# A two-block transformer forward pass: value weights applied to the latent keys ahead of the attention loop, and a new order of weight slots

## The reference, cut to what matters

```python
    c = rmsnorm(ckv, b_kv_norm[l])                      # (b, length, 256)
...
        p = jax.nn.softmax(s, axis=-1)
        o_lat = jnp.einsum('bhqk,bqkc->bqhc', p.astype(g.dtype), g)
        outs.append(jnp.einsum('bqhc,hcd->bqhd', o_lat, w_uv))
    ...
    h = h + jnp.concatenate([o_a, o_b], axis=-1) @ w_out[l]
```

## Time and profile before

| | |
|---|---|
| median of 3 runs | 1381.53 us (1381.42 to 1381.89) |
| the profiled execution: its own time | 1376.42 us |
| its span, first to last instruction | 1374.5 us |
| mean granted TensorE clock | 0.934 |
| PE busy | 1218.1 us (89% of the span) |
| DVE, ACT, POOL busy | 441.1, 391.6, 29.8 us |
| read from device memory | 320.09 MB, 235 GB/s over the span |
| attention loop of the first block with what stands around it | about 360 to 420 us |
| expert stages | 807 to 1008 us and 1157 to 1357 us |

### The profile page before, as it was taken

One profiled execution on the slowest core, in us unless ns is written; L12 is line 12 of the kernel. 1 busy time (PEld: TensorE's weight loads), 2 busy tenths in 40 slices (PEclk: granted clock), 3 DMA queues, 4 the chain that ended last, 5 costly groups with the idle time before them and its releaser, 6 DMA issues.

```text
span 1374.5 us, 18357 instructions
## 1 busy us (share of the span) xinstructions
PE 1218.1 (89%) x7770; PEld 928.0 (68%) x7770; DVE 441.1 (32%) x882; ACT 391.6 (28%) x751; POOL 29.8 (2%) x44
## 2 busy tenths in 40 slices
PE   5999999999999799999989979877789897987776
PEld 3999998877578799999775745433258584452233
DVE  4444544240630544455355121000023713110002
ACT  4333343132541443333145221000113513110002
POOL 0000000100010000000020000000001100000000
PEclk9999999999879899999997989997899998999887
DMA  9455453622102355544230789999976525999993
GB/s 379 169 180 183 159 180 123 228 102 93 62 1 92 142 187 189 187 165 174 92 153 1 311 354 422 423 423 422 423 306 271 218 93 220 422 424 422 422 424 144
DMA packets 44903, 322.43 MB, mean 235 GB/s; under 512 B 5144, under 2 KB 5400, under 8 KB 6672
## 3 DMA queue, kind: packets, MB, share of 16 engines
q1 hardware_dynamic: 43440, 314.45, 57.8%
q0 software_dynamic: 688, 3.69, 0.8%
q10 hardware_dynamic: 688, 3.05, 0.6%
HBM read 320.09 MB, written 3.16 MB: 235 GB/s over the span
## 4 chain that ended last, share of the span: by engine, by line
PE 69%; DMA 20%; DVE 7%; ACT 2%; issue 1%; SPq 1%; ACTq 0%; DVEq 0%
PE bank L1070 10%; PE bank L1027 9%; PE bank L1028 9%; PE bank L1029 9%; DMA ring<-in_stream 8%; PE bank L1037 6%; DMA arena<-in_stream 6%; DMA xn<-in_stream 4%; PE bank L1475 3%; PE bank L1454 3%; PE bank L1104 3%; DMA sm<-in_stream 2%; PE bank L1080 2%; PE bank L1494 2%; PE bank L990 2%
## 5 line engine op out<-in xcount | busy, mean ns | idle before, releaser
L1027 PE MATMUL bank<-r_hi,w_hi 128*128 128x272 f32 (+1 forms) x1056 | 303.0, 287 | 17.1 <-DVE r_lo L1595 13.9
L1028 PE MATMUL bank<-r_lo,w_hi 128*128 128x272 f32 (+1 forms) x1056 | 303.9, 288 | 0.0
L1029 PE MATMUL bank<-r_hi,w_lo 128*128 128x272 f32 (+1 forms) x1056 | 302.9, 287 | 0.0
L1027 PEld LDWEIGHTS bank<-r_hi,w_hi 128*128 128x128 f32 x1056 | 201.7, 191 | 18.4 <-issue 18.3
L1589 DVE TENSOR_TENSOR w_lo<-ring,w_hi 128x2048 fp32r<-128x2048 f32 x66 | 151.3, 2292 | 177.1 <-ACT w_hi L691 177.1
L1029 PEld LDWEIGHTS bank<-r_hi,w_lo 128*128 128x128 f32 x1056 | 201.6, 191 | 0.0
L1028 PEld LDWEIGHTS bank<-r_lo,w_hi 128*128 128x128 f32 x1056 | 200.8, 190 | 0.0
L691 ACT ACTIVATE w_hi<-ring 128x2048 fp32r<-128x2048 f32 x66 | 126.1, 1912 | 143.1 <-PE bank L1029 138.6
L1070 PE MATMUL bank<-xn,ring 128*128 128x256 f32 (+1 forms) x624 | 143.0, 387 | 8.1 <-DVE xn L1580 8.1
L1070 PEld LDWEIGHTS bank<-xn,ring 128*128 128x128 f32 x624 | 118.4, 192 | 30.8 <-issue 12.0
L1926 DVE TENSOR_TENSOR arena<-arena,bank 128x256 f32<-128x256 f32 x16 | 6.7, 421 | 247.8 <-ACT arena L930 247.8
(11 more groups left out here) (299 smaller groups left out, 1216.7 us busy)
## 6 DMA issues: line engine op xcount, KB each, us to landing
ring<-in_stream SPq DMA_DIRECT2D x160, 1024.0 KB, 4.9
arena<-in_stream SPq DMA_DIRECT2D x68, 1024.0 KB, 26.1
sm<-in_stream SPq DMA_DIRECT2D x18, 1024.0 KB, 26.8
G<-in_stream SPq DMA_DIRECT2D x10, 1024.0 KB, 24.8
w_ukv<-in_stream SPq DMA_DIRECT2D x10, 1024.0 KB, 26.0
sq<-in_stream SPq DMA_DIRECT2D x10, 1024.0 KB, 26.6
xn<-in_stream SPq DMA_DIRECT2D x10, 1024.0 KB, 26.3
mixT<-in_stream SPq DMA_DIRECT2D x8, 1024.0 KB, 26.6
```

The lines of the kernel that those rows point to most:

```text
L1027: mm(dst, hi, r_hi[:, k, 0:T], start=first, stop=False)
L1028: mm(dst, hi, r_lo[:, k, 0:T], start=False, stop=False)
L1029: return mm(dst, lo, r_hi[:, k, 0:T], start=False, stop=last)
```

## The change

Two edits. **Values:** `w_uv` is laid out as two tiles of 512 columns, one per half of the latent, with all four heads side by side. Ahead of the loop PE multiplies the latent keys of each token tile with it (L1255 of the new file: two matmuls of 512 columns per token tile, for the tiles 0, 2 and 1 into the banks 6, 5 and 7). The third waits for the save of the last projection, which lies in bank 7. ACT saves them as `vlat`, [tokens, 512]. A kind-b unit then has one column tile, and its output `obT` is already the head's output, which `down` reads in place of `mixT`; the matmuls and copies behind the loop are gone. **Slots:** the table is made per layer by `moe_slots(first)`, with the ring slots counted from that of the layer's first projection chunk. For layer 1 it is the old table.

```diff
@@ -156,7 +156,7 @@
         w_uk = w_ukv1[:, 0:1024].rearrange("p (h n) -> p h n", h=4)
-        w_uv = w_ukv1[:, 1024:2048].rearrange("p (h c n) -> p h c n", h=4, c=2)
+        w_uv = w_ukv1[:, 1024:2048].rearrange("p (c n) -> p c n", c=2)
         SM = 2048 + 1024 + 256 + 288
@@ -215,13 +215,13 @@
         qlT = carve("qlT", at["iw"], 8, T1)
-        ctok = carve("ctok", at["qlT"], 3, BDC)
-        selb = carve("selb", at["ctok"], 3, T1)
-        olT = carve("olT", at["selb"], 8, T1)
-
-        ql_sq = olT
-
-        W0 = at["olT"]
+        selb = carve("selb", at["qlT"], 3, T1)
+        vlat = carve("vlat", at["selb"], 3, 512)
+        ql_sq = carve("ql_sq", at["selb"] + 768, 8, T1)
+        obT = ql_sq[:, 4:8, :]
+        assert at["vlat"] <= at["selb"] + 768 + 4 * T1
+
+        W0 = at["ql_sq"]
         s_sb = carve("s_sb", W0, 2, 2, 272)
@@ -297,9 +297,14 @@
         assert len(slot_at) == NS2
-        moe_slot = ([S_G, S_UKV, S_AR, S_AR + 1, 4, 5, S_SQ, S_XN, S_SM] + [S_AR + j for j in range(2, 6)]
-                    + [0, 1, 2, 3, S_AR + 6, S_MIX, S_ROOT])
-        assert sorted(moe_slot) == list(range(NS2))
+
+        def moe_slots(first):
+
+            ring_slot = [(first + j) % NS for j in range(NS)]
+            order = ([S_G, S_UKV, S_AR, S_AR + 1] + ring_slot[4:6] + [S_SQ, S_XN, S_SM] + [S_AR + j for j in range(2, 6)]
+                     + ring_slot[0:4] + [S_AR + 6, S_MIX, S_ROOT])
+            assert sorted(order) == list(range(NS2))
+            return order
 
@@ -418,8 +423,8 @@
                 bias=None,
-                v=[lambda k, nk, c=c: ctok[0:nk, k, P * c:P * c + P] for c in range(2)], base=0, M=P, s=s_sb, a=a_sb, aT=aT,
-                out=olT[:, 2 * h:2 * h + 2, P * i:P * i + nq])
+                v=[lambda k, nk: vlat[0:nk, k, P * h:P * h + P]], base=0, M=P, s=s_sb, a=a_sb, aT=aT,
+                out=obT[:, h, P * i:P * i + nq])
 
@@ -477,7 +482,7 @@
             else:
-                j = moe_slot[(n - MOE_AT[l]) % NS2]
+                j = moe_slots(slot_of[A_IN2[l]])[(n - MOE_AT[l]) % NS2]
                 turn = 0
@@ -762,8 +767,6 @@
                 src = bank[6 + g % 2][b:b + M, 0:nq * len(u["v"])]
-                if len(u["v"]) == 2:
-                    src = src.rearrange("p (c n) -> p c n", c=2)
                 if u["kind"] == "a":
@@ -825,18 +828,16 @@
                 if g == 1:
-                    act.wait_ge(S("ctok_ready"), 1)
-                    link(copy(ctok[:, 0:2, :], bank[6].rearrange("p (t n) -> p t n", t=2), ACT.Copy))
-                    copy(ctok[0:16, 2, :], bank[5][0:16, 0:BDC], ACT.Copy).then_inc(S("ctok_saved"), 1)
+                    for t, b in ((0, 6), (2, 5), (1, 7)):
+                        nq = TOKENS1[t][1]
+                        act.wait_ge(S("vlat_ready"), 2 if t == 2 else 1 if t == 0 else 3)
+                        copy(vlat[0:nq, t, :], bank[b][0:nq, :], ACT.Copy).then_inc(S("vlat_saved"), 1)
 
...
             steps(SEG_1, (save_T, 2), (save_o, 3), (exps, 0), (save_last, 0), (subln_root, 3))
-            for h in range(BH):
-                act.wait_ge(S("ob_ready"), h + 1)
-                copy(mixT[:, 4 + h, 0:T2], bank[4 + h][:, 0:T2], ACT.Copy).then_inc(S("ob_saved"), 1)
             squares(2)
@@ -1028,13 +1029,13 @@
 
-            def down(at, c0, c1, turned, ready):
+            def down(at, c0, c1, src, ready):
 
...
                     def part(d, f):
-                        return mm(y_half(d), w[:, f, P * d:P * d + P], mixT[:, (2 * c + f + turned) % KT, 0:T2],
+                        return mm(y_half(d), w[:, f, P * d:P * d + P], src(2 * c + f),
                                   start=c == 0 and f == 0 and d % 2 == 0, stop=c == 3 and f == 1, skip_group_check=True)
@@ -1245,11 +1246,14 @@
             pe.wait_ge(S("spread_used"), SPREAD_USED[11])
-            for t, (q0, nq) in enumerate(TOKENS1):
-                dst = bank[6][:, 256 * t:256 * t + 256] if t < 2 else bank[5][0:nq, 0:256]
+            pe.wait_ge(S("wu_loaded"), 32)
+            for t, b in ((0, 6), (2, 5), (1, 7)):
+                q0, nq = TOKENS1[t]
+                if t == 1:
+                    pe.wait_ge(S("proj_saved"), U1)
                 for c in range(2):
-                    ins = nc.tensor.transpose(dst[:, P * c:P * c + P], uT[:, 12 + c, q0:q0 + nq], ident)
-            ins.then_inc(S("ctok_ready"), 1)
+                    ins = mm(bank[b][0:nq, :], uT[:, 12 + c, q0:q0 + nq], w_uv[:, c, :], start=(c == 0), stop=(c == 1))
+                ins.then_inc(S("vlat_ready"), 1)
             pe.wait_ge(S("spread_used"), SPREAD_USED[12])
@@ -1260,7 +1264,7 @@
                 if g == 1:
-                    pe.wait_ge(S("ctok_saved"), 1)
+                    pe.wait_ge(S("vlat_saved"), 3)
                 turn(g)
@@ -1282,13 +1286,8 @@
             steps(SEG_1, (scores_1, 0), (turn_1, 2), (pv_1, 3), (subln, 3))
-            pe.wait_ge(S("o_saved"), SEG_B[1])
-            pe.wait_ge(S("wu_loaded"), 32)
-            for h in range(BH):
-                for c in range(2):
-                    ins = mm(bank[4 + h][:, 0:T2], w_uv[:, h, c, :], olT[:, 2 * h + c, 0:T2], start=(c == 0), stop=(c == 1))
-                ins.then_inc(S("ob_ready"), 1)
-            down(A_OUT1, 0, 4, 0, lambda k: [("subln_done", AH)] if k == 0 else [("ob_saved", k - 3)] if k >= 4 else [])
+            down(A_OUT1, 0, 4, lambda k: mixT[:, k, 0:T2] if k < AH else obT[:, k - AH, 0:T2],
+                 lambda k: [("subln_done", AH)] if k == 0 else [("o_saved", SEG_B[0] + k + 1)] if k >= AH else [])
             norm(2)
@@ -1380,14 +1379,17 @@
 
+                def mixed(k):
+                    return mixT[:, (k + 4) % KT, 0:T2]
+
                 def first_half(g):
...
                         pe.wait_ge(S("pool_saved"), 2 * (l + 1))
-                        down(A_OUT2[l], 0, 2, 4, lambda k: [])
+                        down(A_OUT2[l], 0, 2, mixed, lambda k: [])
 
                 steps(SEG_M[l], (scores, 0), (pool_mix, 0), (first_half, 1), (turn_m, 2), (pv, 3))
-                down(A_OUT2[l], 2, 4, 4, lambda k: [("o_saved", SEG_M[l][1] - 7 + 2 * (k - 4) + 1)])
+                down(A_OUT2[l], 2, 4, mixed, lambda k: [("o_saved", SEG_M[l][1] - 7 + 2 * (k - 4) + 1)])
                 for d in range(KT):
@@ -2050,7 +2052,7 @@
         "wuk": i["b_w_uk"][0].transpose(1, 0, 2),
-        "wuv": i["b_w_uv"][0].reshape(4, 2, P, P).transpose(2, 0, 1, 3),
+        "wuv": i["b_w_uv"][0].reshape(4, 2, P, P).transpose(2, 1, 0, 3),
         "small2": np.stack(small2),
```

## The result

The changed kernel takes 1372.7 us (median of 9 runs, 1367.32 to 1379.05), the kernel before in the same comparison 1381.89 (9 runs, 1379.12 to 1387.63). The ratio is 0.9932, 95% interval 0.9905 to 0.996, so 9.4 us less with 5.5 to 13 possible. **Forecast: 1375.3, in a range of 1368.5 to 1381.5, faster.** A ratio compares the runs within 1.5% of a kernel's fastest; medians are of all runs.

The account below looks back on a forecast made before the run. Expert stages wait for weights, most of the rest for PE and DVE. Compute terms +4.4, -6.25, -4.2 (-6.0), clock +1.5 and branch wait -1.7 gave -6.2 us: 1370.2 profiled, 1375.3 us as median, range 1368.5 to 1381.5.

Parts of the forecast that it names:

- Part 1: Ahead of block 1's attention loop: six transposes go, six 512-column matmuls (5.18 us) come, all on the path; +4.4 us.
- Part 2: In block 1's attention loop: kind-b units' value matmuls halve, with nothing gained at units 10 and 12; -6.25 us.
- Part 3: Behind the loop: eight matmuls and a save go, so the output projection starts right behind the last unit; -4.2 us.
- At most 0.3 us of new waiting: End of the loop: unit 15 needs ACT's save of its turned tile, which ends about together with PE's work.
- it was at full clock before and after: Block 1's loop: PE at half clock through 374 to 396 us, at full clock on either side.
- rival 1: Block 1: half clock lasts from its fall up to the output projection; +3.3 in all, 1384.8 us, slower; chance 0.12.
- The clock: Block 1's loop: work before the fall is later, so nearly two more steps at half clock; +1.5 us, -5 to +11.
- rival 4: The clock helps: half rate ends some steps sooner, or the second block gains; -5 more, 1370.3 us; chance 0.13.
- Part 4: Layer 0 slot order: nine transfers leave earlier, so PE's wait at the branch falls from 3.04 towards 1.34; -1.7 us.
- rival 3: Expert stage: early transfers shorten it, nine chunks being 22 us; 1353 us; chance 0.02.
- rival 2: Layer 0: the slot order does nothing and the branch waits as before; -4.5, 1377.0 us; chance 0.13.
- up to 3.8 either way: Second block's attentions: a 5 us shift moves where the clock falls; taken as 0, kept for the range.

Follow-up runs that it names:

- e10: Changed kernel with the six 512-column matmuls ahead of the loop run twice; 1387.17 us, ratio 0.9986 to the kernel before.
- e6: Changed kernel with every kind-b value matmul run twice, so the value work costs PE what it did before; 1377.47 us, ratio 0.9967 to the kernel before.
- e11: Kernel before with seven 512-column matmuls filling PE's wait for the router in each layer; 1380.95 us, ratio 1.0 to the kernel before.
- e8: Changed kernel with five and seven 128-column matmuls filling PE's waits ahead of turns 12 and 14; 1373.81 us, ratio 0.9937 to the kernel before.
- e9: Changed kernel with PE's waits ahead of turns 12 and 14 and for the router of each layer filled; 1366.62 us, ratio 0.9891 to the kernel before.
- e1: Kernel before with the value edit alone, slot table as before; 1379.21 us, ratio 0.9968 to the kernel before.
- e3: Both edits, the changed kernel run once more beside its parts; 1374.93 us, ratio 0.9947 to the kernel before.
- e12: Both edits with nothing else, the changed kernel run again in the last group; 1373.16 us, ratio 0.9936 to the kernel before.

## Why the prediction was right, point by point

- **Part 1, +4.4.** Right: 5.65 us for the six wide matmuls (5.18 forecast, 0.94 each where 0.864 was taken from L1037), and turn 0 comes 4.8 us later after the start of this work (4.15 between the two profiles, since it began 0.7 us sooner). e10 showed that all of it is on the path.
- **Part 2, -6.25.** Right in mechanism: with the work back, e6 needs 63.6 us from turn 0 to the projection and not 51.8. Units 10 and 12 are hidden as forecast. Units 14 and 15 take 3.45 us where 2.02 was forecast, since they ran mostly at half clock.
- **Part 3, -4.2.** Right: the projection starts directly behind the last unit. "At most 0.3 us of new waiting" holds for unit 15, but not for what is late next: the waits for DVE ahead of turns 12 and 14 are 1.22 and 1.67 us, where the old loop in e11 has 0.40 and 0.62. The 0.8 and 1.0 us that they grew by are the hidden work of units 10 and 12: the sum rightly gave it no worth, and did not ask what PE does with the time.
- **The step that failed** is "it was at full clock before and after", carried over to the new loop. Behind those two waits the clock falls (413 us in the changed kernel), and about seven of the projection's first 32 matmuls run at 1.2 GHz. That is +2.7 us, which the sum lacks. It is a small form of rival 1, placed one stage later than I looked for it. e8 and e9 take it away by filling the waits. What else can bring a fall there, as in e6 and e11, is open.
- **The clock, +1.5 with -5 to +11.** The sign was wrong on average. Half clock from 368 to 399 us in the profiled execution is the +1.5 case. From turn 0 to the projection it needs 51.8 us where before needs 58.9; parts 2 and 3 make -10.45 of that, so the clock's term was +3.3. But half of the eight profiles hold the full clock and need 41.2 us, which makes the term -7.3, past the -5 of the range. That is rival 4, which had 0.13. The projection started 10.9 us earlier on average, where -4.5 was forecast, and about 2 us of this come from which executions were profiled.
- **Part 4, -1.7.** Right in mechanism, a little large: 2.06 against 3.04 us in the profiled pair, -1.3 over the profiles. 0 for the transfers beside the attention is right too: e1's layer 0 attention takes 34.8 us without transfers, and e3's 34.7 with them. The expert stage itself kept its length, so rival 3 falls. So does rival 2.
- **Missing altogether:** the second wait in layer 1, 3.0 us and 3.9 with what follows. I looked at where transfers move and not at where instructions move. And the -3.3 in layer 0's attention was named as "up to 3.8 either way" and left at 0.

So 1375.3 against 1372.7 is in part luck. The parts that were read from rows are right, but four errors of 2.7 to 6.4 us nearly cancel: the clock ahead of the projection (-6.4 beside the forecast), the half clock in it (+2.7), the second wait (+3.9) and the attention of layer 0 (-3.3).

## What to carry to other kernels

Where an engine that waits is also one whose clock can fall, a removed piece of work must be followed to the waits that it opens, and to the first long stretch behind them: behind two waits of 1.22 and 1.67 us the next stage took 3 us more than with the waits filled. In the 28 branches of this study the wait was shortest where no bulk transfer ran while the branch was taken, and an edit that changes the number of instructions ahead of it can add or remove a wait of 3 us behind it. Judge changes below 1% by stages and over several profiles of either kernel, taken in executions of the same kind: here one kind gave 3 to 5 us in a stage and the other 16 to 19. A gain shown in one stage (4.4 us in e8) can be gone two stages later.

## What was not expected of the hardware

- The same loop of the same program (e12 and the changed kernel) runs at full clock in one execution and at half in another, 141 against 98 matmul records in 28 us, and the one at full clock had run at half clock for a stretch some 100 us ahead of the loop, and the other had not.
- PE stood still 2.95 to 3.18 us between two records of neighbouring instructions behind a branch, with no releaser that the profile shows, and only at one of the instruction counts tried.
- The wait at a branch is 1.17 to 2.26 us with DMA engines nearly idle, 2.93 to 3.22 while weights land, and 4.50 when PE arrives 3.0 us earlier in that landing.
- Why layer 0's attention gets 0.90 of the clock after a slower projection and 0.78 after a faster one (e8, e9) is open. No run changed that stretch alone.
